# Two narrow weight jobs joined into one of 72 columns, first token tiles turned by halves, in a two-layer four-mixer block

## The reference

```
h = rmsnorm(x, n_pre_mix)
proj = h @ w_in
(gdn_qkv, gdn_z, gdn_a, gdn_b, dswa_qkv, sb_qkv, ret_qk, ret_v, ret_g, gates) = split_cols(proj, COL_SIZES)
...
beta = jax.nn.sigmoid(gdn_b)            # gdn_a, gdn_b: 4 columns each, the gates of mixer a
...
qb, kb, vb = [t.reshape(B, S, 9, 64) for t in jnp.split(dswa_qkv, 3, axis=-1)]   # mixer b: 9 heads of 64
...
mixed = (g_a * y_a + g_b * y_b + g_c * y_c + g_d * y_d) @ w_o
x = x + rmsnorm(mixed, n_post_mix)
h2 = rmsnorm(x, n_pre_mlp)
f = jnp.square(jax.nn.relu(h2 @ w_mlp_in)) @ w_mlp_out
```

## Time and profile before

| what | value |
| --- | --- |
| median of 3 runs | 2466.92 us |
| the profiled execution | 2465.01 us, its span 2463.2 us |
| PE busy | 2388.1 us, 97% |
| POOL busy | 1312.7 us, 53% |
| DVE busy | 926.0 us, 38% |
| ACT busy | 782.8 us, 32% |
| mean granted TensorE clock | 0.991 of full speed |

### The profile page before, as it was taken

How to read it: one execution, slowest core, us unless ns; L and a number is a source line. 1 busy time by engine, 2 the same in 40 slices (tenths; PEclk the granted TensorE clock), 3 DMA queues, 4 the chain that set the end, 5 groups by cost and what they waited for, 6 DMA issues and landing times.

```text
span 2463.2 us, 29730 instructions
## 1 busy us (share of the span) xinstructions
PE 2388.1 (97%) x11872; PEld 1953.2 (79%) x11872; DVE 926.0 (38%) x1396; ACT 782.8 (32%) x1549; POOL 1312.7 (53%) x748
## 2 busy tenths in 40 slices
PE   8999999999998999999999999999999989999998
PEld 7798877787876788888887888777778767888887
DVE  3663324344444341123356532253345343311223
ACT  5533326213125241122254442352231352311221
POOL 5511663555552556677664126545556525666774
PEclk9999999999999999999999999999999999999999
DMA  4300331322230233323222013213221213333221
GB/s 153 95 27 27 87 93 43 111 86 86 62 90 28 96 95 101 94 94 100 81 83 81 18 36 94 85 52 103 86 87 55 88 37 94 103 100 97 95 95 68
DMA packets 107672, 197.45 MB, mean 80 GB/s; under 512 B 8592, under 2 KB 21008, under 8 KB 107152
## 3 DMA queue, kind: packets, MB, share of 16 engines
q1 hardware_dynamic: 106384, 189.27, 25.0%
q10 hardware_dynamic: 1152, 6.29, 0.8%
HBM read 193.44 MB, written 2.10 MB: 79 GB/s over the span
## 4 chain that ended last, share of the span: by engine, by line
PE 85%; DVE 8%; ACT 5%; issue 2%; POOL 1%; DMA 0%; POOLq 0%; DVEq 0%; SPq 0%; ACTq 0%
PE big L1607 62%; PE mix L1607 8%; PE mix L1744 5%; PE big L1920 1%; DVE c_lo L1394 1%; PE mix L1888 1%; PE mix L1814 1%; PE mix L1987 1%; ACT scr L986 1%; PE mix L2078 1%; PE mix L1899 1%; PE mix L1707 1%; DVE scr L1241 0%; DVE scr L1406 0%; POOL ring_lo L560 0%
## 5 line engine op out<-in xcount | busy, mean ns | idle before, releaser
L558 POOL TENSOR_SCALAR ring_hi<-stage 128x1024 fp32r<-128x1024 f32 (+2 forms) x372 | 383.4, 1031 | 1094.4 <-PE big L1607 1024.4
L560 POOL TENSOR_TENSOR ring_lo<-stage,ring_hi 128x1024 fp32r<-128x1024 f32 (+2 forms) x372 | 930.8, 2502 | 31.0
L1607 PE MATMUL big<-h_hi,ring_hi 128*128 128x512 f32 (+1 forms) x1904 | 725.4, 381 | 5.4 <-DVE h_lo L1127 2.5
L1607 PE MATMUL big<-h_hi,ring_lo 128*128 128x512 f32 (+1 forms) x1904 | 715.3, 376 | 0.0
L1607 PE MATMUL big<-h_lo,ring_hi 128*128 128x512 f32 (+1 forms) x1904 | 715.2, 376 | 0.0
L1607 PEld LDWEIGHTS big<-h_hi,ring_hi 128*128 128x128 f32 x1904 | 358.9, 188 | 78.0 <-issue 8.4
L1607 PEld LDWEIGHTS big<-h_lo,ring_hi 128*128 128x128 f32 x1904 | 358.5, 188 | 66.4
L1607 PEld LDWEIGHTS big<-h_hi,ring_lo 128*128 128x128 f32 x1904 | 359.0, 189 | 64.9 <-issue 1.9
L1555 DVE TENSOR_TENSOR h_lo<-scr,h_hi 128x1024 fp32r<-128x1024 f32 x64 | 84.8, 1325 | 248.3 <-ACT h_hi L1045 248.3
L1607 PE MATMUL big<-ring_hi,h_hi 128*128 128x512 f32 x448 | 174.9, 390 | 1.8 <-POOL ring_lo L560 1.8
L1607 PE MATMUL big<-ring_hi,h_lo 128*128 128x512 f32 x448 | 174.3, 389 | 0.0
(11 more groups left out here) (257 smaller groups left out, 2880.7 us busy)
## 6 DMA issues: line engine op xcount, KB each, us to landing
stage<-in_w_in SPq DMA_DIRECT2D x168, 512.0 KB, 3.5
stage<-in_w_mlp_in SPq DMA_DIRECT2D x64, 512.0 KB, 3.6
stage<-in_w_mlp_out SPq DMA_DIRECT2D x64, 512.0 KB, 3.3
stage<-in_w_o SPq DMA_DIRECT2D x16, 512.0 KB, 3.3
stage<-in_w_br_a SPq DMA_DIRECT2D x8, 512.0 KB, 3.9
stage<-in_w_br_c SPq DMA_DIRECT2D x8, 512.0 KB, 3.3
stage<-in_w_br_d SPq DMA_DIRECT2D x8, 512.0 KB, 3.3
stage<-in_w_br_b SPq DMA_DIRECT2D x8, 512.0 KB, 3.8
```

What stands on the lines that cost most here:

```text
L558: nc.gpsimd.tensor_scalar(rH[jw][0:pp, r, 0:kk, 0:job.n], w, 1.0, 0.0, ALU.mult, ALU.add).then_inc(sem("w_hi"), 1)
L560: nc.gpsimd.tensor_tensor(rL[jw][0:pp, r, 0:kk, 0:job.n], w, f32(rH[jw][0:pp, r, 0:kk, 0:job.n]), ALU.subtract).then_inc(sem("w_ready"), 1)
L1607: ins_ = MM(o_, a_, r_, start=s0, stop=s1)
```

## The change

- `aab` and `bv8` become one job `aab` of 72 columns from a new array `w_ab`: the 64 value columns first, then the 8 gate columns. Its single bank gives ACT two copies: the 8 gate rows (now on partitions 64 to 71), then the 64 value rows, in their strided order, into a place `bV8` of their own until mixer b. PE's transposes of the gates wait for the first copy (`a_ab`) only.
- `bv8` is gone: per layer four units of 64 columns (24 matmuls), 4 DMAs and 8 POOL instructions fewer; one value copy less at L954's place.
- The six value groups run in another order: the ninth head first (its bank is `mix` 3), then the tiles of `bv`; the last one, after the fill, is now the fourth tile of `bv`.
- The counter `n` advances one less before `gateb0`, so job tiles from `gateb0` on lie one `big` bank earlier, up to the end of the layer. The fixed banks of the token-major tiles stay.
- The first two token tiles are normed, turned and split by halves: half 0 of both tiles, then half 1 of both (`turn_at`). PE turns all of it before its first job matmul, as before.
- Smaller edits: some constants go and their weight loads read one column with stride 0 (`ones_r`, the last block of `rot_r`, the selectors of L2078). `idb`, `strictb` lie in scratch and are made anew in each layer, with one TENSOR_TENSOR more. The two constant DMAs shrink from 2112 to 1920 and from 640 to 520 columns.

```diff
-VT = ((0, 0, P, 0, 0), (1, 0, DH, 0, P), (1, DH, P, 1, 0), (2, 0, P, 1, DH), (3, 0, P, 2, 0), (4, 0, DH, 2, P))
+VT = ((4, 0, DH, 2, P), (0, 0, P, 0, 0), (1, 0, DH, 0, P), (1, DH, P, 1, 0), (2, 0, P, 1, DH), (3, 0, P, 2, 0))
...
-    add("aab", "w_in", C_AB, P, DM, "T", "h")
+    add("aab", "w_ab", 0, DH + 8, DM, "T", "h")
...
-    add("bv8", "w_in", C_DSWA + 1152 + 512, DH, DM, "T", "h")
...
+        def turn_at(tag, t, hf):
+
+            return 2 * hf + t if tag == "pre1" and layer[0] == 0 and t < 2 else 2 * t + hf
...
-                normed("pre1", 0)
-                normed("pre1", 1)
+                normed("pre1", 0, (0,))
+                normed("pre1", 1, (0,))
                 act.wait_ge(*upto("small_loaded", 16))
-                split_hi("pre1", LN1, 0)
-                split_hi("pre1", LN1, 1)
+                for hf in range(2):
+                    for t in range(2):
+                        split_hi("pre1", LN1, t, range(4 * hf, 4 * hf + 4))
+                    if hf == 0:
+                        normed("pre1", 0, (1,))
+                        normed("pre1", 1, (1,))
...
-            big_free(A(g_ab, ps[0:8, :], ACT.Copy), ("aab", 0))
+            A(g_ab, ps[DH:DH + 8, :], ACT.Copy).then_inc(sem("a_ab"), 1)
+            big_free(A(bV8.rearrange("p (r l) -> p r l", r=DIL[2]), ps[0:DH, :].rearrange("p (l r) -> p r l", r=DIL[2]), ACT.Copy), ("aab", 0))
...
-            for t in range(5):
+            for t in range(4):
                 value_raw(t)
...
-            if l == 0:
-                V.tensor_copy(idb[:, :], ident).then_inc(sem("c_bias"), 1)
-
-                V.tensor_scalar(strictb[:, :], strict, -NEG, NEG, ALU.mult, ALU.add).then_inc(sem("c_bias"), 1)
+            V.tensor_copy(idb[:, :], ident).then_inc(sem("c_bias"), 1)
+            TT(strict, triu, ident, ALU.subtract).then_inc(sem("c_bias"), 1)
+            dve.wait_ge(*upto("c_bias", 2))
+            V.tensor_scalar(strictb[:, :], strict, -NEG, NEG, ALU.mult, ALU.add).then_inc(sem("c_bias"), 1)
...
-                turned("pre1", 0)
-                turned("pre1", 1)
+                for hf in range(2):
+                    for t in range(2):
+                        turned("pre1", t, (hf,))
...
-                    done(MM(ps[:, :], f32(ones_r[:, :]), q_sq[:, i % 4, :], start=True, stop=True), ("l2", i))
+                    done(MM(ps[:, :], f32(ones_r[:, 0:1]).to_broadcast((P, P)), q_sq[:, i % 4, :], start=True, stop=True), ("l2", i))
...
-                big_freed(pe, ("aab", 0))
+                pe.wait_ge(*upto("a_ab", 1))
...
-            do("bv8")
...
-                big_freed(pe, ("bv", t) if t < 4 else ("bv8", 0))
+                big_freed(pe, ("bv", t) if t < 4 else ("aab", 0))
+                raw = bX[:, (t + 1) % 4, :] if t < 4 else bV8
```

More of the change, by code:

```diff
@@ L96, in shape_constants @@
     first = (k <= p + P) & (k >= P)
-    sel = np.zeros((P, 3 * DH), np.float32)
-    for h in range(3):
+    sel = np.zeros((P, 2 * DH), np.float32)
+    for h in range(2):
         sel[h, h * DH:(h + 1) * DH] = 1.0
@@ L109, in shape_constants @@
     consts = np.concatenate(
-        [one(p == c), one(c >= p), one(c > p), *levels,
+        [one(p == c), one(c >= p), *levels,
          neg(np.concatenate([first, near], 1)), neg(c <= p),
-         neg((c <= p) & ((p - c) % 4 == 0)), sel, rotation(8), rotation(32), -one(c <= p), -one(c > p), -one(c + p >= 0)], 1)
+         neg((c <= p) & ((p - c) % 4 == 0)), sel, rotation(8), rotation(32), -one(c <= p), -one(c > p), -one(c + p >= 0)[:, 0:8]], 1)
     return np.ascontiguousarray(consts.astype(np.float32))
@@ L357, in hybrid_kernel @@
         consts = sb("consts", CRD)
-        ones_r, rot_r = sb("ones_r", P, F32R), sb("rot_r", 5 * P, F32R)
-        idb, strictb = sb("idb", P, BF16), sb("strictb", P, BF16)
+        ones_r, rot_r = sb("ones_r", 8, F32R), sb("rot_r", ROT, F32R)
         lw = sb("lw", LEND)
         st = sb("st", 328)
-        scr = sb("scr", 19968)
-        scr_at = nc.sbuf_base - 4 * 19968
+        scr = sb("scr", SCR)
+        scr_at = nc.sbuf_base - 4 * SCR
+        idb, strictb = (nc.alloc_sbuf_tensor_at(n, [P, P], BF16, offset=scr_at + 4 * at) for n, at in (("idb", 19456), ("strictb", 19520)))
         c_hi = nc.alloc_sbuf_tensor_at("c_hi", [P, 5 * S], F32R, offset=scr_at + 4 * C_HIGH)
@@ L603, in x_root, with normed @@
                 A(p_y[:, t:t + 1], p_t[:, t:t + 1], ACT.Exp, scale=-0.5).then_inc(sem(f"{tag}_y"), 1)
-            def normed(tag, t):
+            def normed(tag, t, hfs=range(2)):
                 act.wait_ge(*upto(f"{tag}_nw", 2 * t + 2))
-                for hf in range(2):
+                for hf in hfs:
                     cs = slice(hf * 512, hf * 512 + 512)
@@ L944, in value_raw @@
             def value_raw(t):
-                key = ("bv", t) if t < 4 else ("bv8", 0)
+                key = ("bv", t)
                 ps = big_wait(act, key)
[L948 to L951, removed]
+                act.wait_ge(*upto("b_rope", t + 6))
                 parts = [(r0, r1, DIL[g]) for tile, r0, r1, g, _ in VT if tile == t]
@@ L1215, in vector_layer @@
                 newton(p_y, p_t, p_h, "pre1", 1)
-                split_lo("pre1", LN1, 0)
-                split_lo("pre1", LN1, 1)
+                for hf in range(2):
+                    for t in range(2):
+                        split_lo("pre1", LN1, t, range(4 * hf, 4 * hf + 4))
                 for t in (2, 3):
@@ L1653, in done, with turned @@
                 ins_.then_inc(sem(home(key)[1]), 1)
-            def turned(tag, t):
-                for hf in range(2):
+            def turned(tag, t, hfs=range(2)):
+                for hf in hfs:
                     ps = tile_of((tag, t, hf))
-                    pe.wait_ge(*upto(f"{tag}_h", 2 * t + hf + 1))
+                    pe.wait_ge(*upto(f"{tag}_h", turn_at(tag, t, hf) + 1))
                     for q in range(4):
@@ L1862, in head_means @@
                     pe.wait_ge(*upto("an_sq", h + 1))
-                    done(MM(ps[:, :], f32(ones_r[:, :]), g_sq[:, h % 2, :], start=True, stop=True), ("an", h))
+                    done(MM(ps[:, :], f32(ones_r[:, 0:1]).to_broadcast((P, P)), g_sq[:, h % 2, :], start=True, stop=True), ("an", h))
             do("gatea1", between=lambda i: head_means(*((0, 1), (2, 3), (), ())[i]))
@@ L1905, in stick_sums @@
                     else:
-                        i = MM(c_bank[u][:, P:], rot_r[:, 4 * P:5 * P], part[:, u - 3, 0:384], start=False, stop=True, skip_group_check=True)
+                        i = MM(c_bank[u][:, P:], rot_r[:, 4 * P:4 * P + 1].to_broadcast((P, P)), part[:, u - 3, 0:384], start=False, stop=True, skip_group_check=True)
                 i.then_inc(sem("c_sum"), 1)
```

49 lines of the change are left out of this document (27 added, 22 removed).

## The result

| kernel | median | runs | lowest to highest |
| --- | --- | --- | --- |
| before | 2466.92 us | 6 | 2465.72 to 2467.32 |
| changed | 2475.59 us | 6 | 2474.43 to 2477.45 |

The ratio is 1.0037, with a 95% interval of 1.0026 to 1.0047: the change makes the kernel slower, by 8.7 us. The forecast was 2477, range 2467 to 2483. The profiled execution took 2475.5 us. Its span is 2473.7 us against 2463.2, a difference of 10.5 us; it is more than 8.7 because the profile of the kernel before lies 1.9 us under its median and this one does not.

The account below looks back on a forecast made before the run. PE, busy 97% of the span, was taken to bound the kernel. Per layer 0.4 + 1.7 + 1.0 + 1.9 + 0.4 = 5.4, twice 10.8, less 0.5: +10.3 us, giving 2475.3 profiled, 2477 as median; range 2467 to 2483.

Parts of the forecast that it names:

- The removed job hid a wait: Behind bv: the removed 5.5 us matmul stream per layer covered ACT's wait for the last rotation; at best 2.0 us gained.
- POOL beside DVE: Behind bv: POOL's 1024-wide units hold up DVE's two-input SBUF operations and so the last rotation; +0.4 us per layer.
- The stepping: DVE and POOL worked through in turn from 683.90: last rotation ends at 701.8, fill starts at 703.2, 0.3 us later.
- That ACT's order caps the gain: Fifth transpose group behind bv needs a bank ACT empties only after its last raw value copy; at best 2.0 us gained.
- The clock: After PE's stand from about 697.5 to 702.8, 3.4 us at half clock in the matmuls; +1.7 us per layer.
- The banks at `o0`: Tiles 0 and 1 of o0 each wait 0.5 us for DVE to free their shifted banks; +1.0 us per layer.
- The banks at `up0`: PE stands 2.1 us at up0 for a shifted bank, 0.2 come back; +1.9 us per layer, plus 0.4 for low clock.
- The start: Start of the program: norming by halves lets PE reach a tile at about 17.3 instead of 17.80; -0.5 us once.
- Costed at nothing: The 64-row ACT copy, stride-0 weight loads, small strictb instructions, smaller DMAs and the joined job's matmuls were taken as 0.

Follow-up runs that it names:

- pool_held: The changed kernel, but POOL waits for the last rotation (b_rope 9) before it splits the second unit of gateb0: 2467.57 us, ratio 1.0009.
- new_banks_in_before: The kernel before, with only the bank counter advanced by three ahead of gateb0, giving gateb0 to up7 the changed kernel's banks: 2471.74 us, ratio 1.0022.
- kept_busy: The changed kernel with 7 and 11 further matmuls of 512 tokens put into PE's two waits behind bv: 2479.25 us, ratio 1.0041.
- pool_held_in_before: The kernel before, with POOL waiting for the last rotation before the second unit of gateb0: 2464.82 us, ratio 0.9996.

## Why the prediction was right

- **The removed job hid a wait.** Right, and the main step. PE stands 4.6 us of the 5.5 that went. One of the two waits is missing from the prediction, though: it had PE go through four groups and stand before the fifth alone, and PE already stood 1.87 us before the fourth, for the bank of the last rotation. The sum does not change by it, since the fifth group's wait ends last.
- **POOL beside DVE.** Right in cause (`pool_held`) and size. The stepping had the last rotation end at 701.8; it ended at 704.2 in a profile whose PE was 2.4 us late ahead of `bv`, which is 701.8 again. The first fill was forecast 0.3 later and came 0.7 later. The difference lies behind the rotation: from its end to the fill the stepping left 1.4 us, though the prediction's own working for the kernel as it was (699.33 to 700.9) makes it 1.6, and it took 1.8, because the fifth group took 0.76 us at low clock where the earlier trace rows have 0.41. The step of +1.0 at the second unit of `bv` was not foreseen. DVE's chain did not move with it (its half of L1465 at 683.95 answers to 681.69 before, 2.3 us later), so by these rows PE would without it only have stood longer.
- **That ACT's order caps the gain.** Right: with DVE undisturbed the fill began at 702.1 and PE still waited for ACT. The removal gave nothing as the kernel was ordered, and nearly all of its 11 us when the fill was put over ACT's late copy and POOL was held.
- **The clock.** Right in kind and about in size: 2.65 and 1.33, forecast 1.7 each. The low stretch was 6.8 us long, not 3.4, and only the part that fell on matmuls cost: half of 5.0 and of 2.3 us on the fill, and 0.35 in the fifth group of each layer, which the ledger has in the row above.
- **The banks at `o0`.** Forecast +1.0, measured +1.2 per layer.
- **The banks at `up0`.** Forecast +1.9, and 0.4 for the clock. The wait is 2.15, the start 2.2 later, but 0.9 come back, half at the next transposes and half at those 7 us later, where I gave 0.2 in all, and no low clock followed in this execution: +1.3. Mis-sized, 1.0 too high per layer.
- **The start.** -0.7 for -0.5; that the halves give it is not shown.
- **Costed at nothing.** Mixer d's stretch (460 to 660) takes 0.53 and 0.59 us more, about as much in every profile of the changed family, and nothing in `new_banks_in_before`. The mean distance of matmuls rises from 0.2270 to 0.2275 us. I had put the rewritten weight loads at 0. Which edit does it was not tried.

The mechanism was right, but the closeness of the number is in part luck. The terms at `bv`, `o0` and `up0` with the clock sum to 10.4 us against a forecast of 10.8, and in that sum `up0` was 2.0 too high where the fill, the clock and `o0` were 1.6 too low together. Mixer d's 1.1 us had no term. The low clock elsewhere happened to cancel between the layers (+1.58, -1.79). The forecast of +10.3 was for the profiles, which differ by 10.5; the medians differ by 8.7.

## What to carry to other kernels

Before a job is taken out, look at what is late behind it; here it covered 4.6 us of waits, and the removal paid only when the next unit was moved over them and POOL was kept off DVE's last chain. When an allocator hands out banks in turn, taking one out moves all that follow: compare each fixed place with its new tenant. And a helper engine that runs ahead is not free when its instructions hold up those of the chain that ends last (here 3.25 us for 1.07); let it wait for that chain.

## What the runs showed of the hardware that was not expected

**The clock behind a stand is not settled by the stand.** PE stands about 3.3 us between 115 and 119 in each kernel. The window of 3.4 us behind it, in the changed kernel and in `kept_busy`:

```profile
119.40:122.80 3.40, 3.40 (x16) 3.30 (x16) 1.16 (x2) 0.00 (x0) 0.00 (x0) 0.50 0.02 5
...
119.40:122.80 3.40, 3.40 (x22) 2.98 (x21) 2.85 (x4) 0.00 (x0) 1.75 (x2) 1.00 0.03 7
```

Up to this place the two programs are the same, and PE resumes at 118.52 in both, after 3.32 and 3.33 us. One is granted 1.2 GHz for 6.8 us, the other 2.4 GHz throughout; at 130 us they are 2.6 us apart. With several such stands in each layer this is a likely source of the scatter of a kernel's runs. The Trainium skill (TensorE: Matmul & The Clock Gate, "What's actually happening") calls the count of slow matmuls at a kernel's start run-variable. These rows do not show the start; they show the like for a stand in the middle.

**A tie between two engines can cost a microsecond.** In the kernel before, DVE's L1435 and POOL's L558 both start at 671.34, and DVE takes 0.69. In the changed kernel, with POOL first by 0.07 us:

```profile
673.77 1.05 POOL L564 TENSOR_SCALAR ring_hi<-stage 128x1024 fp32r<-128x1024 f32 x1
673.84 1.51 DVE L1444 TENSOR_TENSOR o_lo<-scr,o_hi 128x512 fp32r<-128x512 f32 x1
675.28 2.89 DVE L1465 TENSOR_TENSOR scr<-scr 128x512 f32<-128x512 f32 x1
678.91 0.50 PE L1616 MATMUL big<-h_hi,ring_hi 128*128 128x512 f32 x1 [0.66 <-ACT scr L949]
```

From then on DVE and POOL take turns the other way round, and PE waits 0.66 us in `bv`. The kernel before stands on the edge here. `new_banks_in_before` and `pool_held_in_before` run the same program up to here in layer 1 and the same unit in layer 2. In these three kernels the two engines start within 0.03 us of each other in all six cases. DVE keeps its 0.69 us in three of them and takes 1.58 or 1.59, with the step of 1.0 us behind it, in the other three. In all nine profiles of kernels with the change POOL is first by 0.05 to 0.07 us, in both layers, and the step is always there. So the change makes certain what before happened now and then; which of its edits moves the two engines was not tried.
